# Delta rule's levels, solves and recurrence one tick later in the hand-written order, its output's turn two ticks later

## The reference, cut to what matters

```python
L = where(strict, einsum("bhncd,bhnsd->bhncs", kb, k) * exp(diff), 0)
sol = triangular_solve(eye + L, [v * beta, kb * exp(gc)])      # u, w
def step(S, inp):                                             # for each chunk
    v_new = u_c - w_c @ S
    o = qg_c @ S + a_c @ v_new
    S = S * d_c + kd_c.T @ v_new
```

## Time and profile before

| what | before |
|---|---|
| median of 3 runs | 860.32 us (859.57 to 860.8) |
| profiled execution | 859.1 us |
| its span in the trace | 857.3 us |
| TensorE busy | 840.5 us, 98% |
| weight loads busy | 773.4 us, 90% |
| VectorE busy | 623.7 us, 73% |
| ScalarE busy | 509.0 us, 59% |
| GpSimd busy | 74.8 us, 9% |
| DMA | 148.94 MB, mean 174 GB/s |

### The profile page before, as it was taken

The page is one execution under the profiler, slowest core; times in us unless marked ns, Lnnn a source line. Parts: engine busy times, 40 slices in busy tenths (PEclk is TensorE's granted clock), DMA queues, the critical chain, the costliest instruction groups (busy, mean ns, idle before and its releaser), DMA issues. The chain is left out here.

```text
span 857.3 us, 14484 instructions
## 1 busy us (share of the span) xinstructions
PE 840.5 (98%) x5732; PEld 773.4 (90%) x5732; DVE 623.7 (73%) x1122; ACT 509.0 (59%) x830; POOL 74.8 (9%) x76
## 2 busy tenths in 40 slices
PE   8999999999999999999999899999999999999996
PEld 7999999999989999999999699899899888788885
DVE  6887987998877757665665979787456577775765
ACT  6575778665377656655566787554544545554453
POOL 0100003001020211111112100500000010000000
PEclk9999999999999999999999999999999999999999
DMA  8747443457455655555555463744232243365541
GB/s 305 238 169 278 156 140 123 156 189 295 148 193 177 230 189 174 194 196 189 177 175 172 147 215 124 286 165 147 99 100 99 99 148 123 127 222 191 196 148 49
DMA packets 40587, 148.94 MB, mean 174 GB/s; under 512 B 4524, under 2 KB 5192, under 8 KB 39880
## 3 DMA queue, kind: packets, MB, share of 16 engines
q1 hardware_dynamic: 40520, 148.02, 50.7%
HBM read 146.93 MB, written 1.08 MB: 173 GB/s over the span
## 5 line engine op out<-in xcount | busy, mean ns | idle before, releaser
L1795 DVE TENSOR_TENSOR t_wl<-t_raw,t_wh 128x1024 fp32r<-128x1024 f32 x259 | 314.7, 1224 | 98.7 <-ACT t_wh L1268 97.5
L1268 ACT ACTIVATE t_wh<-t_raw 128x1024 fp32r<-128x1024 f32 x259 | 271.6, 1058 | 112.6 <-PE bank L625 59.3
L620 PE MATMUL bank<-t_hh,t_wh 128*128 128x256 f32 x1144 | 330.5, 289 | 1.5 <-DVE t_wl L1795 1.2
L622 PE MATMUL bank<-t_hh,t_wl 128*128 128x256 f32 x1144 | 323.6, 283 | 0.0
L621 PE MATMUL bank<-t_hl,t_wh 128*128 128x256 f32 x1144 | 323.6, 283 | 0.0
L620 PEld LDWEIGHTS bank<-t_hh,t_wh 128*128 128x128 f32 x1144 | 219.1, 192 | 4.9 <-DVE t_wl L1795 2.0
L621 PEld LDWEIGHTS bank<-t_hl,t_wh 128*128 128x128 f32 x1144 | 219.2, 192 | 0.9
L622 PEld LDWEIGHTS bank<-t_hh,t_wl 128*128 128x128 f32 x1144 | 219.1, 192 | 0.0
L625 PE MATMUL bank<-t_wh,t_br 128*128 128x512 f32 x384 | 123.4, 392 | 0.0
L1810 DVE SCALAR_TENSOR_TENSOR t_arena<-bank,t_par,t_arena 128x255 f32<-128x255 f32 (+2 forms) x184 | 75.2, 474 | 45.1 <-ACT t_arena L1273 44.7
L625 PE MATMUL bank<-t_wh,t_hh 128*128 128x512 f32 x224 | 91.5, 408 | 3.2 <-DVE t_wl L1795 3.2
(11 more groups left out here) (147 smaller groups left out, 831.4 us busy)
## 6 DMA issues: line engine op xcount, KB each, us to landing
t_raw<-in_ws SPq DMA_DIRECT2D x259, 512.0 KB, 3.9
t_br<-decay SPq DMA_DIRECT2D x1, 2048.0 KB, 8.8
t_arena<-in_post SPq DMA_DIRECT2D x3, 512.0 KB, 6.5
t_arena<-gates SPq DMA_DIRECT2D x1, 1536.0 KB, 10.7
t_x<-in_xin SPq DMA_DIRECT2D x2, 512.0 KB, 5.0
t_bd<-in_bd SPq DMA_DIRECT2D x1, 1024.0 KB, 8.4
t_x<-in_xtok SPq DMA_DIRECT2D x1, 1024.0 KB, 6.4
t_arena<-in_mem SPq DMA_DIRECT2D x1, 1024.0 KB, 8.5
```

What stands on the lines that cost most here:

```text
L620: e.matmul(o, wh, xh, start=first, stop=False, skip_group_check=True)
L622: return e.matmul(o, wl, xh, start=False, stop=last, skip_group_check=True)
L1268: e.activation(WH[q % NS][:, :], RAW[q % NR][:, :], ACT.Copy, bias=0.0, scale=1.0).then_inc(*hi.now(q))
L1795: e.tensor_tensor(WL[q % NS][:, :], RAW[q % NR][:, :], WH[q % NS][:, :].bitcast(F), SUB).then_inc(*lo.now(q))
```

## The change

In `dn_lane` of TensorE, ScalarE, VectorE and GpSimd each tick from the first level to the end of the recurrence is one higher; the last turn on TensorE goes from 209 to 211; on VectorE the root goes from 206 to 207, the scaling from 208 to 209, the gate from 210 and 211 to 212 and 213. What comes before the levels (ticks up to 179) stays, and so do all other lanes. The instructions and their waits are the same.

```diff
@@ TensorE, dn_lane
-                        yield from walk.until(180 + 3 * level + (hf if level < 2 else 0))
+                        yield from walk.until(181 + 3 * level + (hf if level < 2 else 0))
...
-                    yield from walk.until((182, 185, 187)[level])
+                    yield from walk.until((183, 186, 188)[level])
...
-                    yield from walk.until(188 + 3 * n)
+                    yield from walk.until(189 + 3 * n)
...
-                    yield from walk.until(189 + 3 * n)
+                    yield from walk.until(190 + 3 * n)
...
-                    yield from walk.until(190 + 3 * n)
+                    yield from walk.until(191 + 3 * n)
...
-                    yield from walk.until(194 + hf)
+                    yield from walk.until(195 + hf)
...
-                        yield from walk.until(197 + 2 * c)
+                        yield from walk.until(198 + 2 * c)
...
-                    yield from walk.until(198 + 2 * c)
+                    yield from walk.until(199 + 2 * c)
...
-                yield from walk.until(209)
+                yield from walk.until(211)
@@ ScalarE, dn_lane: the levels, solves, u and w, vn likewise, and
-                        yield from walk.until(199 + 2 * c)
+                        yield from walk.until(200 + 2 * c)
@@ VectorE, dn_out_lane
-                yield from walk.until(206)
+                yield from walk.until(207)
...
-                yield from walk.until(208)
+                yield from walk.until(209)
...
-                    yield from walk.until(210 + i)
+                    yield from walk.until(212 + i)
@@ GpSimd, dn_lane
-                    yield from walk.until(194 + c)
+                    yield from walk.until(195 + c)
```

## The result

**866.24 us** (median of 6 runs, 864.96 to 867.18) against 860.25 us of the kernel before beside it (6 runs, 859.46 to 861.34): ratio 1.0065, 95% interval 1.0055 to 1.0075. Slower, as forecast, but by 6.0 us where the forecast had 2.5, and 1.4 us above the top of the range. The profiled execution took 866.26 us, its span 864.5 us, 7.2 us more than before.

A forecast was written before the change was run, and what follows sets the result against it. TensorE, busy for 98% of the span, was taken as the bound, so only its waits count. Terms -0.24 + 0.62 - 0.99 + 3.79 - 0.57 - 0.10 = +2.5 us on 860.32 gave 862.8 us, range 861.0 to 864.8.

The forecast's parts named there:

- The three waits of before: TensorE's waits at ticks 180 (ScalarE), 189 and 209 (both VectorE) go: -0.24, -0.99 and -0.57 us.
- Tick 184, +0.62: TensorE's turn at tick 184 waits for ScalarE's drain of the squared matrix, late after softmax exponentials: new wait +0.62 us.
- Tick 193, +3.79: Second solve's product waits for VectorE's masks behind two softmaxes, a gate and a split: new wait +3.79 us.
- The clock is no variable so far: Granted clock is 1.00 even where TensorE is busy only 3.40 us of 5, so no clock term in the sum.
- the case of a low clock behind the new wait: Rival: a 1.2 GHz stretch follows the new wait, 1.8 us more, 864.6 us in all; chance 5%.
- Tick 205: Recurrence's last difference comes after a softmax at tick 205, with half a microsecond left: cost 0.
- thin cover: Rival: bank at tick 197, inverse at 195 and difference at 205 give way, 0.5 to 1.5 us more; chance 10%.
- the prediction's own signs of being wrong: Mask ahead of a softmax, large wait below 2 us, or another wait over half a microsecond between ticks 194 and 213.
- The tick 197 bank: Bank for the next chunk, emptied by ScalarE's drains from tick 196, free some 0.3 us before TensorE asks: cost 0.
- Changes of operand, -0.10: Small float32 work between units costs about 0.1 us per interruption; one tick fewer has it: -0.1 us, bounds 0 and -0.2.
- The sum: All terms, -0.24 + 0.62 - 0.99 + 3.79 - 0.57 - 0.10 = +2.5 us, giving 862.8 us; chance 68%.
- The two rivals: Low clock behind the new wait (864.6 us, chance 5%) and thin covers giving way (863.3 to 864.3 us, 10%).

The follow-up runs named there:

- the filler: Changed kernel plus 14 matmuls of 512 columns, result unread, on TensorE ahead of the late product of tick 193: 863.47 us, ratio 1.0035 to the kernel before.
- the earlier mask: Changed kernel with VectorE making the second solve's masks at tick 191, behind both softmaxes but ahead of gate and split: 861.68 us, ratio 1.0021.
- the repeat: Changed kernel as it is, timed again beside the kernel before: 865.12 us (6 runs), ratio 1.0060.
- the copy a tick later: Changed kernel with ScalarE's copy of the last difference at tick 205 instead of 204: 864.78 us, ratio 1.0050.

## Why the prediction was wrong, point by point

- *The three waits of before go* (-0.24, -0.99, -0.57): right, each; the last also alone.
- *Tick 184, +0.62*: 0.63, and 0.69 us shorter once the drain was early. *Tick 193, +3.79*: 3.79. Right in size, place and cause; taking the mask out from behind gate and split shrank it by the 1.75 us that they had been given, and with the window softmax out of its way 0.18 us of it was left.
- **The clock was the step that failed.** "The clock is no variable so far" rested on a stretch whose idle time is one piece of 1.59 us; a second, of 1.65 us, comes some 4.7 us later (TensorE's timeline of before, below). Neither is half of the 3.79 us that the prediction added, and the case of a low clock behind the new wait was named, priced at 1.8 us, and given 5%. It cost 1.7 us in the trace, and the filler and the earlier mask each gave it back. The argument against it, that the drain of the last matmul covers part of the wait, was worth 0.16 us of 3.79. The price of 1.8 us was right in size by luck: it was half of a product of 3.57 us, but the same product took 3.13 us in the trace with the filler, not half of 3.57, and no row ties its length to how long the clock stays low. A forecast whose largest term is a single wait more than twice as long as any in the trace can't lean on the trace's clock. The Trainium skill (TensorE: Matmul & The Clock Gate, section "HAM oscillation — how this bites in real kernels") has it that waits between bursts of matmuls can throttle the engine again. The trace agrees: behind 3.63 us of idle time the mean granted clock was 0.66 over 5 us.

```profile
477.46 0.50 PE L625 MATMUL bank<-t_wh,t_hh 128*128 128x512 f32 x1 [1.59 <-DVE t_wl L1795]
...
482.12 0.50 PE L625 MATMUL bank<-t_wh,t_hh 128*128 128x512 f32 x1 [1.65 <-DVE t_wl L1795]
```

- **Tick 205 was mis-sized**: "kept at 0, with half a microsecond left". It cost 0.6 us. I had checked when the delta rule's value reaches TensorE, not what is queued behind ScalarE's copy that waits for it. Here that was a split, behind it a VectorE accumulation, behind it the bank of an ordinary unit. That chain has three engines and no link to the delta rule at its end. It was in the list of rivals as a thin cover (a step that comes only just in time), with 10%, and a wait of over half a microsecond between ticks 194 and 213 was one of the prediction's own signs of being wrong; this was such a wait, by a little.
- The tick 197 bank, another thin cover, held in the change; with softmaxes moved it broke at once, for 2.6 us and the clock again.
- *Changes of operand, -0.10*: not measured by itself; what the stage leaves for it and for rounding is -0.14.
- *The sum*: 2.5 forecast + 1.7 clock + 0.6 bank = 4.8, which is the stage's 4.8. The two rivals were treated as excluding each other; both came on top of the main case, and the range was not wide enough for the two together. From the median of that batch another 1.2 us remain, 0.3 us from the repeat; the clock at the start and the 0.75 us near 550 us, which come and go among executions of identical code, are of that size, and the mean clocks of the single runs go with it. That they are the whole of it is argued, not shown.

## What to carry to other kernels

Where steps from a hand-written schedule move by one slot, list for every engine what then stands in front of the moved step, and for every wait what stands behind it in the same queue, down to the bank of unrelated work. Price a new long wait twice, by its length and by the slower clock behind it, and let the second be the expected case where the wait is far longer than any in the trace. Here the place of one pair of masks in one engine's list was worth 4.1 us of the stage, more than twice what all the waits that the change removed were worth (1.8).

## What the runs showed that I had not expected

- Idle pieces of TensorE in this kernel: 1.88 us left the clock at 1.00; 2.23, 2.59 and 3.63 us were each followed by 3.4 us at the 1.2 GHz level, which is 1.7 us at half the clock. A longer piece was not followed by a longer stretch. The first three pieces stand in one trace each, the longest in three (the changed kernel twice, and with the copy a tick later); whether the length of the piece alone decides is not shown.
- The same code, before tick 180, differed by up to 3.4 us between traces (end of unit 189 at 600.99 and 604.39), most of it in the first 17 us, while the DMA share was about 1.0. There the granted clock fell back for 0, 3.4 or 6.8 us once it had first risen, and before that first rise the low level shows only in the matmuls' pitch. A difference of under a microsecond in this kernel is read from the stage, not from a median.
